# Tile order, small copies and the decays' chain in the start of a DeltaNet/MoBA block kernel

## The chip, the cores and the metric

The kernel runs on one core of one Trainium2 chip. The metric is the device time of a whole execution in microseconds (us), the median of several runs. The profile is of one execution of the same program.

## What is computed

One decoder block over 256 tokens of 1024 channels, all in float32. `x` is RMS-normalised to `h`, and one projection of `h` gives everything else:

```python
h = rms_norm(x, norm_pre_w)
proj = jnp.einsum('bsd,df->bsf', h, w_in)
qkv_a, z_a, beta_a, dec_a, qkv_b, z_b, gate_logits = ...
qkv_a = jax.nn.silu(causal_depthwise_conv(qkv_a, conv_w))        # 4 taps, per channel
beta = jax.nn.sigmoid(beta_a)
g = -jnp.exp(dn_a_log) * jax.nn.softplus(dec_a + dn_dt_bias)      # the decays
oa = gated_delta_rule(qa, ka, va, g, beta)                        # 8 heads of 128, chunks
ya = rms_norm(oa, dn_onorm_w) * silu(z_a)
ob = moba_attention(qb, kb, vb, rel_bias)                         # 256 tokens: one causal block
yb = ob * silu(z_b)
merged = sigmoid(gates_a) * (ya @ w_branch[0]) + sigmoid(gates_b) * (yb @ w_branch[1])
out = x + rms_norm(merged @ w_out, norm_post_w)
```

## The kernel before

Every large product is made in three parts. Weights and activations are split into a high part, rounded to the fp32r type, and the remainder: `w_hi`, `w_lo`, `h_hi`, `h_lo`. A product is `h_hi w_hi + h_lo w_hi + h_hi w_lo`, three passes over the same bank of PSUM. Weights come in tiles of 128 x 1024 (512 KB), one DMA each on SyncE's queue, into four slots (`raw`). ScalarE makes the high part (`split_hi`), VectorE the remainder (`split_lo`), TensorE does the three passes. A tile is loaded once the remainder of the tile four before it has left its slot.

The whole program is written out by hand, engine by engine, over one counter `S`: `n = S // 3` is the tile, `part = S % 3` the pass. In each step `S` every engine does first `gates(S)` (the small work for beta and decays), then the work on key tiles (`key_front`), and more, and ScalarE ends `part == 1` with the cast of tile `n + 2`, VectorE ends `part == 2` with its remainder. Each engine takes its instructions strictly in that order, and semaphores tie the engines together.

The first sixteen tiles are named by a string. K is a tile of the key projection of one DeltaNet head (8 blocks of 128 rows x 128 columns of `w_in`, out 128 channels x 256 tokens), V one of the attention's value projection (two blocks of 128 rows x 512 columns, for two of the eight parts of `h`; four V tiles make one group of 512 columns, in banks `bE` and `bF`).

```python
FIRST = "KVKKVKKVKKVKVVVV"
```

A K tile with index `j` among the K tiles goes to bank `j % 2` (`third`), and `bank_free` makes TensorE wait until the taps of key tile `j - 2` have read that bank: `pe.wait_ge(s_tap, 3 * (j - 1))`. For a key tile, ScalarE copies the bank times the fourth tap to `acc`, VectorE adds three shifted taps (`conv`, line 974): two in the step in which the tile is done, the third in the next. ScalarE's tanh and a last step on VectorE (line 987) give `kT_all`, which TensorE later transposes (`key_tokens`, the table `TOKENS` says at which `S`).

The start: `x` is normalised, 16 transposes (line 1266) turn it to channels x tokens in PSUM (`x_T`, `h` in eight parts), ScalarE rounds each part to `h_hi` (line 652), VectorE makes `h_lo` (line 926). `first_tile` (line 1332) is tile 0, here a K tile: 24 matmuls of 256 columns in an order that follows those parts, with the last four transposes among them. Its cast is done by VectorE (`first_hi`), its remainder by GpSimd. Tile 1's cast follows on ScalarE behind all eight roundings, then the cast of the small weights `wbd` (16 columns for beta and decays); VectorE has the first half of tile 1's remainder, then the remainder of `wbd`, then the other half.

Beta and decays: TensorE's `gates` at `S == 4` (16 matmuls, line 1291), a copy on ScalarE to `bd_T` (line 662), two transposes at `S == 6`. At `S == 7` VectorE has `bd_lo`, `bd`, `gt[:, 1]` and the copy `brow` (lines 943 to 951), ScalarE tanh, absolute value, two exponentials and a logarithm, which needs another table (lines 665 to 673), and GpSimd the chain between them (lines 525 to 541). VectorE sums at `S == 8` (line 960), and TensorE makes the cumulative sums at `S == 11` (lines 1307 to 1309).

## Time and profile before

| | |
|---|---|
| median of 3 runs | 354.02 us (353.72 to 354.14) |
| the profiled execution | 354.62 us |
| its span in the profile | 352.8 us |
| TensorE matmul busy | 345.2 us, 98% |
| VectorE | 269.7 us, 76% |
| ScalarE | 220.5 us, 62% |
| GpSimd | 61.0 us, 17% |
| HBM read | 60.41 MB, 176 GB/s over the span with what is written |

The span runs from the first to the last instruction of the program; the execution's time holds 1.8 us more around it. In the rows, PE is TensorE's matmuls, PEld its weight loads, DVE VectorE, ACT ScalarE, POOL GpSimd. Busy time of matmuls is modelled at their ends, and neighbours overlap in the records; where one matmul follows the other, the chain of waits shows what each group really adds.

### The profile page before, as it was taken

What the parts mean: (1) busy time and instruction counts of PE and PEld (TensorE: products, weight loads), DVE (VectorE), ACT (ScalarE), POOL (GpSimd) and SP (SyncE); (2) the same over time, 40 slices, a digit from 0 to 9 for tenths busy, and PEclk for the clock granted to TensorE, in tenths of its full rate; (3) what the DMA queues carried; (4) which work ended last, traced back from release to release, by engine and by line L of the source; (5) the groups of instructions that cost most, each with busy time, mean ns of one, the idle gap of its engine ahead of it and who ended that gap; (6) DMA issues with size and microseconds to landing.
All of it is one profiled execution on the core that took longest, in us unless ns stands there. A gap on an engine that the chain in (4) does not pass through costs nothing.

```text
span 352.8 us, 7457 instructions
## 1 busy us (share of the span) xinstructions
PE 345.2 (98%) x2753; PEld 332.2 (94%) x2753; DVE 269.7 (76%) x565; ACT 220.5 (62%) x499; POOL 61.0 (17%) x112
## 2 busy tenths in 40 slices
PE   8999999999999999999999999999999999999993
PEld 6889998999999999999999999999999999999882
DVE  4869897499986868978789797887967557588644
ACT  4778895455466667686866867677667655444421
POOL 2535535500033000300203011030200201000011
PEclk9999999999999999999999999999999999999999
DMA  7958948996799564655555565655555556775703
GB/s 233 274 140 225 304 125 201 236 289 171 209 248 218 134 180 126 163 133 153 146 150 149 131 170 129 171 132 146 143 159 143 171 158 181 208 240 186 260 32 119
DMA packets 100321, 62.48 MB, mean 177 GB/s; under 512 B 4692, under 2 KB 95230, under 8 KB 100286
## 3 DMA queue, kind: packets, MB, share of 16 engines
q1 hardware_dynamic: 98030, 58.59, 60.6%
q0 software_dynamic: 1072, 3.04, 3.0%
q10 hardware_dynamic: 1184, 0.39, 0.5%
q8 instruction: 22, 0.36, 0.4%
q14 instruction: 13, 0.11, 0.1%
HBM read 60.41 MB, written 1.59 MB: 176 GB/s over the span
## 4 chain that ended last, share of the span: by engine, by line
PE 97%; DVE 1%; issue 1%; POOL 0%; ACT 0%; DVEq 0%; POOLq 0%; ACTq 0%
PE banks L1347 67%; PE banks L1365 6%; PE banks L1560 6%; PE banks L1256 2%; PE banks L1445 1%; PE banks L1422 1%; PE banks L1462 1%; PE banks L1451 1%; PE banks L1332 1%; PE banks L1291 1%; PE banks L1507 1%; PE banks L1479 1%; PE banks L1483 1%; PE banks L1512 1%; PE banks L1487 1%
## 5 line engine op out<-in xcount | busy, mean ns | idle before, releaser
L890 DVE TENSOR_TENSOR w_lo<-raw,w_hi 128x1024 fp32r<-128x1024 f32 x102 | 124.1, 1218 | 44.4 <-ACT w_hi L637 43.9
L637 ACT CAST w_hi<-raw 128x1024 fp32r<-128x1024 f32 x103 | 107.5, 1047 | 10.0 <-PE banks L1560 5.5
L1347 PE MATMUL banks<-h_hi,w_hi 128*128 128x256 f32 x568 | 81.4, 286 | 0.0
L1347 PE MATMUL banks<-h_hi,w_lo 128*128 128x256 f32 x568 | 76.6, 278 | 0.0
L1347 PE MATMUL banks<-h_lo,w_hi 128*128 128x256 f32 x568 | 76.6, 278 | 0.0
L1347 PEld LDWEIGHTS banks<-h_hi,w_hi 128*128 128x128 f32 x568 | 71.0, 189 | 0.3
L1347 PEld LDWEIGHTS banks<-h_hi,w_lo 128*128 128x128 f32 x568 | 69.9, 188 | 0.0
L1347 PEld LDWEIGHTS banks<-h_lo,w_hi 128*128 128x128 f32 x568 | 69.9, 188 | 0.0
L974 DVE SCALAR_TENSOR_TENSOR acc<-banks,vec,acc 128x255 f32<-128x255 f32 (+2 forms) x72 | 34.5, 479 | 4.0 <-ACT acc L761 2.1
L587 POOL TENSOR_TENSOR so<-so,rnq 128x2 f32<-128x2 f32 x8 | 2.6, 328 | 162.8 <-ACT junk L828 162.8
L761 ACT ACTIVATE acc<-banks,vec 128x256 f32<-128x256 f32 x16 | 7.6, 474 | 18.7 <-PE banks L1347 18.7
L1347 PE MATMUL banks<-y_hi,w_hi 128*128 128x256 f32 x128 | 17.7, 281 | 0.0
L1347 PE MATMUL banks<-y_hi,w_lo 128*128 128x256 f32 x128 | 17.2, 277 | 0.0
L1347 PE MATMUL banks<-y_lo,w_hi 128*128 128x256 f32 x128 | 17.2, 277 | 0.0
L1347 PEld LDWEIGHTS banks<-y_hi,w_hi 128*128 128x128 f32 x128 | 15.8, 188 | 0.0
L1347 PEld LDWEIGHTS banks<-y_hi,w_lo 128*128 128x128 f32 x128 | 15.8, 188 | 0.0
L1347 PEld LDWEIGHTS banks<-y_lo,w_hi 128*128 128x128 f32 x128 | 15.8, 188 | 0.0
L1560 PE MATMUL banks<-w_hi,h_lo 128*128 128x512 f32 x32 | 12.6, 395 | 0.0
L1560 PE MATMUL banks<-w_lo,h_hi 128*128 128x512 f32 x32 | 12.5, 392 | 0.0
L1560 PE MATMUL banks<-w_hi,h_hi 128*128 128x512 f32 x32 | 12.4, 389 | 0.0
L765 ACT COPY bT<-banks 128x256 f32<-128x256 f32 x16 | 5.9, 371 | 9.3 <-PE banks L1347 9.2
L744 ACT CAST h_hi<-th_E 128x256 fp32r<-128x256 f32 x8 | 3.2, 406 | 12.1 <-DVE th_E L1190 12.1
(243 smaller groups left out, 548.3 us busy)
## 6 DMA issues: line engine op xcount, KB each, us to landing
raw<-in_w_in_dram SPq DMA_DIRECT2D x79, 512.0 KB, 4.0
raw<-in_w_branch_dram SPq DMA_DIRECT2D x16, 512.0 KB, 3.7
raw<-in_w_out_dram SPq DMA_DIRECT2D x8, 512.0 KB, 3.3
xin<-in_x_dram SPq DMA_DIRECT2D x2, 512.0 KB, 3.9
th_E<-g_rows POOLq DMA_DIRECT2D x2, 512.0 KB, 6.6
bias<-bias_rows POOLq DMA_DIRECT2D x1, 1024.0 KB, 8.2
raw<-in_x_dram SPq DMA_DIRECT2D x2, 512.0 KB, 4.4
out_dram<-xin SPq DMA_DIRECT2D x4, 256.0 KB, 2.0
```

Of the source, the lines that this page charges most:

```text
L637: nc.scalar.copy(w_hi[:, t % SLOTS, :], raw[:, t % SLOTS, :]).then_inc(s_hi, 1)
L761: ac(acc[:, t, :], ps, ACT.Copy, scale=tap(CONV - 1, 2 * t, h)).then_inc(s_tap0, 1)
L765: nc.scalar.copy(bT[:, t - 2, :], ps).then_inc(s_bT, 1)
L890: v.tensor_tensor(w_lo[:, t % SLOTS, cols], raw[:, t % SLOTS, cols], w_hi[:, t % SLOTS, cols].bitcast(F32), ALU.subtract).then_inc(s_lo, 1)
L974: v.scalar_tensor_tensor(out=acc[:, a, i:], in0=ps[:, 0:SEQ - i], scalar=tap(CONV - 1 - i, w, h), in1=acc[:, a, i:], op0=ALU.mult, op1=ALU ...
L1256: mm(bank[6][:, 0:SEQ], acc[:, 0, 0:P], acc[:, 0, :], start=True, stop=True)
L1291: last = mm(bA[0:4 * HEADS, 0:SEQ], wbd2[:, k, :], h_part[:, k, :], start=k == 0 and h_part is h_hi, stop=k == KT - 1 and h_part is h_lo)
L1332: last = mm(ps, (w_lo if which[1] == "l" else w_hi)[:, 0, P * k:P * k + P], (h_lo if which[0] == "l" else h_hi)[:, k, :], start=i == 0, st ...
L1347: last = mm(ps, w, r, start=part == 0 and k == 0, stop=part == 2 and k == KT - 1)
L1365: last = mm(((bE, bF), (bB, bE))[group][c], left, right, start=q == 0 and kk == 0 and part == 0, stop=q == 3 and kk == 1 and part == 2)
L1422: last = mm((bA, bC)[j % 2][:, P * c:P * c + P], k, k, start=True, stop=True)
L1560: last = mm(bank[2 + 2 * c + e], m[:, k, P * c:P * c + P], w[:, (OUT0 + k) % SLOTS, 512 * e:512 * e + 512], start=k == 0 and m is m_hi and ...
```

## The change

Tiles 0 and 1 change places: tile 0 is now a V tile, tile 1 the first K tile. `first_tile` makes the V tile's twelve matmuls of 512 columns, which need two of the eight parts of `h`, with the last six transposes among them; ten stand ahead. The eight parts in PSUM lie in other banks. The cast of tile 1 stands on ScalarE between the sixth and the seventh rounding, and VectorE's remainder of `wbd` ahead of tile 1's remainder. The constants `ones` and `tri` are loaded behind the fourth tile of weights and not ahead of the third. Key tile 0's work begins at `S == 6` and not at `S == 3`, its transposes move from `S == 10` to 12. The copy to `bd_T` is written at `S == 4` ("the projection's copy"), ahead of the cast of tile 3, together with the exponential of `alog`. GpSimd's chain of nine instructions on the decays is now VectorE's, in `gates` at `S == 7`. The diff, with one line around each piece:

```diff
@@ -51,7 +51,7 @@
-FIRST = "KVKKVKKVKKVKVVVV"
+FIRST = "VKKKVKKVKKVKVVVV"
 K_TILES = [n for n, kind in enumerate(FIRST) if kind == "K"]
@@ -69,7 +69,7 @@
-TOKENS = {10: 0, 16: 1, 19: 2, 24: 3, 27: 4, 32: 5, 35: 6, 41: 7}
+TOKENS = {12: 0, 16: 1, 19: 2, 24: 3, 27: 4, 32: 5, 35: 6, 41: 7}
 SIM = {28: 0, 29: 1, 30: 2, 31: 3, 36: 4, 37: 5, 42: 6, 43: 7}
@@ -216,7 +216,7 @@
-        x_T = [bank[(1, 2, 3, 5, 6, 7)[k % 6]][:, SEQ * (k // 6):SEQ * (k // 6) + SEQ] for k in range(KT)]
+        x_T = [bank[(1, 2, 3, 5, 0)[k % 5]][:, SEQ * (k // 5):SEQ * (k // 5) + SEQ] for k in range(KT)]
@@ -410,16 +410,16 @@
             for half in range(2):
-                part = slice(KT // 2 * half, KT // 2 * half + KT // 2)
-                sp.dma_start(raw[:, 0, :].rearrange("p (k n) -> p k n", k=KT)[:, part], w_tile(COL_K)[:, part]
+                sp.dma_start(raw[:, 0, 512 * half:512 * half + 512], w_in[P * half:P * half + P, COL_VB:COL_VB + 512]
                              ).then_inc((s_w0_in, s_raw[0])[half], 16)
             first_load(1)
-            sp.dma_start(cst[:, P:], consts[:, P:]).then_inc(s_cst, 16)
             sp.dma_start(wbd[:], w_in[:, COL_BD:COL_B].rearrange("(k p) n -> p k n", p=P)).then_inc(s_bd_w, 16)
                 first_load(n)
+                if n == 3:
+                    sp.dma_start(cst[:, P:], consts[:, P:]).then_inc(s_cst, 16)
             for g in range(EARLY):
@@ -518,28 +518,9 @@
-            pool.wait_ge(s_ga, 1)
+            pool.wait_ge(s_ga, 2)
             pool.tensor_scalar(gt[:, 11], gt[:, 0], -0.125, -0.125, ALU.mult, ALU.add).then_inc(s_beta, 1)
             pool.wait_ge(s_beta, 1)
-            pool.wait_ge(s_ga, 3)
-            pool.tensor_scalar(gt[:, 4], gt[:, 3], 1.0, 1.0, ALU.mult, ALU.add).then_inc(s_gs, 1)
-            pool.wait_ge(s_gs, 1)
-            pool.tensor_scalar(gt[:, 6], gt[:, 4], 1.0, -1.0, ALU.mult, ALU.add).then_inc(s_gs, 1)
-            pool.wait_ge(s_gs, 2)
-            pool.tensor_tensor(gt[:, 7], gt[:, 3], gt[:, 6], ALU.subtract).then_inc(s_gs, 1)
-            pool.wait_ge(s_gs, 3)
-            pool.tensor_tensor(gt[:, 8], gt[:, 1], gt[:, 2], ALU.add).then_inc(s_gs, 1)
-            pool.wait_ge(s_gs, 4)
-            pool.tensor_scalar(gt[:, 10], gt[:, 8], 0.5, 0.0, ALU.mult, ALU.add).then_inc(s_gs, 1)
-            pool.wait_ge(s_gs, 5)
-            pool.tensor_tensor(gt[:, 10], gt[:, 10], gt[:, 7], ALU.add).then_inc(s_gs, 1)
-            pool.wait_ge(s_gs, 6)
-            pool.wait_ge(s_ga, 4)
-            pool.tensor_scalar(tiny[:, 24:32], tiny[:, 16:24], -1.0, 0.0, ALU.mult, ALU.add).then_inc(s_gs, 1)
-            pool.wait_ge(s_gs, 7)
-            for c in range(NC):
-                pool.tensor_tensor(gt[:, 7, c], gt[:, 10, c], tiny[:, 24:32], ALU.mult).then_inc(s_gs, 1)
-                pool.wait_ge(s_gs, 8 + c)
             pool.wait_ge(s_brow, 1)
@@ -650,26 +631,27 @@
                 ac(h_hi[:, k, :], x_T[k], ACT.Copy, scale=vec[:, R_PRE + k:R_PRE + k + 1]).then_inc(s_h_hi, 1)
-            sa.wait_ge(s_hi, 1)
-            split_hi(1, 1, 1)
+                if k == 5:
+                    sa.wait_ge(s_hi, 1)
+                    split_hi(1, 1, 1)
             sa.wait_ge(s_bd_w, 16)
-                if S == 5:
+                if S == 4:
                     sa.wait_ge(s_bd_m, 1)
                     nc.scalar.copy(bd_T, bA[0:4 * HEADS, 0:SEQ]).then_inc(s_bd_t, 1)
+                    sa.wait_ge(s_small, 32)
+                    ac(tiny[:, 16:24], alog[:], ACT.Exp).then_inc(s_ga, 1)
                 elif S == 7:
                     ac(gt[:, 2], gt[:, 1], ACT.Abs).then_inc(s_ga, 1)
-                    sa.wait_ge(s_ga, 2)
+                    sa.wait_ge(s_ga, 3)
                     ac(gt[:, 3], gt[:, 2], ACT.Exp, scale=-1.0).then_inc(s_ga, 1)
-                    sa.wait_ge(s_small, 32)
-                    ac(tiny[:, 16:24], alog[:], ACT.Exp).then_inc(s_ga, 1)
-                    sa.wait_ge(s_gs, 1)
+                    sa.wait_ge(s_gs, 4)
                     ac(gt[:, 5], gt[:, 4], ACT.Ln).then_inc(s_ga, 1)
@@ -927,11 +909,11 @@
                     first_hi(1)
-            ve.wait_ge(s_lo, 2)
-            first_lo(1, 0, s_lo)
             ve.wait_ge(s_bd_hi, 1)
                             ALU.subtract).then_inc(s_bd_s, 1)
+            ve.wait_ge(s_lo, 2)
+            first_lo(1, 0, s_lo)
             first_lo(1, 1, s_lo)
@@ -949,10 +931,26 @@
                     v.tensor_copy(brow, bC[0:HEADS, 0:BIAS_W]).then_inc(s_brow, 1)
+                    ve.wait_ge(s_ga, 1)
+                    v.tensor_scalar(tiny[:, 24:32], tiny[:, 16:24], -1.0, None, ALU.mult).then_inc(s_gs, 1)
+                    ve.wait_ge(s_ga, 3)
+                    v.tensor_tensor(gt[:, 8], gt[:, 1], gt[:, 2], ALU.add).then_inc(s_gs, 1)
+                    ve.wait_ge(s_gs, 2)
+                    v.tensor_scalar(gt[:, 10], gt[:, 8], 0.5, None, ALU.mult).then_inc(s_gs, 1)
+                    ve.wait_ge(s_ga, 4)
+                    v.tensor_scalar(gt[:, 4], gt[:, 3], 1.0, None, ALU.add).then_inc(s_gs, 1)
+                    ve.wait_ge(s_gs, 4)
+                    v.tensor_scalar(gt[:, 6], gt[:, 4], -1.0, None, ALU.add).then_inc(s_gs, 1)
+                    ve.wait_ge(s_gs, 5)
+                    v.tensor_tensor(gt[:, 7], gt[:, 3], gt[:, 6], ALU.subtract).then_inc(s_gs, 1)
+                    ve.wait_ge(s_gs, 6)
+                    v.tensor_tensor(gt[:, 10], gt[:, 10], gt[:, 7], ALU.add).then_inc(s_gs, 1)
+                    ve.wait_ge(s_gs, 7)
+                    for c in range(NC):
+                        v.tensor_tensor(gt[:, 7, c], gt[:, 10, c], tiny[:, 24:32], ALU.mult).then_inc(s_gs, 1)
                 elif S == 8:
                     ve.wait_ge(s_ga, 5)
-                    ve.wait_ge(s_gs, 7)
                     for c in range(NC):
@@ -1271,15 +1269,12 @@
             pe.wait_ge(s_pre_xb[0], 1)
-            pe.wait_ge(s_vec, 1)
-            for k in range(4, 6):
-                turn(0, k)
+            turn(0, 4)
             pe.wait_ge(s_pre_x[1], 1)
             pe.wait_ge(s_pre_xb[1], 1)
-            for k in range(4, 6):
-                turn(1, k)
+            turn(1, 4)
@@ -1310,27 +1305,35 @@
-
-                ps = bank[0][:, 0:SEQ]
-                order = ("hh0 hh1 lh0 hh2 lh1 hh3 lh2 hl0 hh4 lh3 hl1 hh5 lh4 hl2 hh6 lh5 hl3 hh7 lh6 hl4 "
-                         "hl5 hl6 hl7 lh7").split()
+                def first_turn(k):
+
+                    pe.wait_ge(s_h_lo, k - 4)
+                    for c in range(NC):
+                        turn(c, k)
+
+                def first_products(kk, left, right):
+
+                    for c in range(NC):
+                        mm((bE, bF)[c], left[:, kk, P * c:P * c + P], right[:, 0, 512 * kk:512 * kk + 512],
+                           start=kk == 0 and left is h_hi and right is w_hi, stop=False)
+
+                pe.wait_ge(s_vec, 1)
                 pe.wait_ge(s_w0_hi, 1)
-                for i, which in enumerate(order):
-                    k = int(which[2])
-                    if which == "hh4":
-                        pe.wait_ge(s_hi, 1)
-                    if which in ("lh0", "lh1"):
-                        pe.wait_ge(s_h_lo, k + 1)
-                        for c in range(NC):
-                            turn(c, 6 + k)
-                    if which[0] == "l":
-                        pe.wait_ge(s_h_lo, k + 1)
-                    else:
-                        pe.wait_ge(s_h_hi, k + 1)
-                    if which[1] == "l":
-                        pe.wait_ge(s_lo, 1 + k // 4)
-                    last = mm(ps, (w_lo if which[1] == "l" else w_hi)[:, 0, P * k:P * k + P],
-                              (h_lo if which[0] == "l" else h_hi)[:, k, :], start=i == 0, stop=i == 23)
+                pe.wait_ge(s_h_hi, 1)
+                first_products(0, h_hi, w_hi)
+                first_turn(5)
+                first_products(0, h_lo, w_hi)
+                pe.wait_ge(s_hi, 1)
+                pe.wait_ge(s_h_hi, 2)
+                first_products(1, h_hi, w_hi)
+                first_turn(6)
+                first_products(1, h_lo, w_hi)
+                first_turn(7)
+                pe.wait_ge(s_lo, 1)
+                first_products(0, h_hi, w_lo)
+                pe.wait_ge(s_lo, 2)
+                for c in range(NC):
+                    last = mm((bE, bF)[c], h_hi[:, 1, P * c:P * c + P], w_lo[:, 0, 512:], start=False, stop=False)
                 last.then_inc(s_tile, 1)
@@ -1342,6 +1345,8 @@
                 for k in range(KT):
+                    if n == 1 and part < 2:
+                        pe.wait_ge((s_h_hi, s_h_lo)[part], k + 1)
                     w = (w_lo if part == 2 else w_hi)[:, slot, P * k:P * k + P]
@@ -1373,6 +1378,8 @@
                     j = K_TILES.index(n)
+                    if j == 0:
+                        pe.wait_ge(s_h_lo, 5)
                     if j >= 2:
                 elif n < HEAD0:
```

VectorE around loop step 7, before (`acc<-banks` are the taps of key tile 0, of 255, 254 and 253 columns; `w_lo` the remainders of tiles 2, 3 and 4):

```order
L890 TENSOR_TENSOR w_lo<-raw,w_hi 128x1024
L974 SCALAR_TENSOR_TENSOR acc<-banks,vec,acc 128x255
L974 SCALAR_TENSOR_TENSOR acc<-banks,vec,acc 128x254
L974 SCALAR_TENSOR_TENSOR acc<-banks,vec,acc 128x253
L890 TENSOR_TENSOR w_lo<-raw,w_hi 128x1024
L987 SCALAR_TENSOR_TENSOR kT_all<-tacc,acc 128x256
L943 COPY bd_lo<-banks 128x32
L945 TENSOR_TENSOR bd<-banks,bd_lo 128x32
L949 TENSOR_TENSOR gt<-bd,dtb 128x8 x2
L951 COPY pt<-banks 8x384
L957 TENSOR_TENSOR gt<-gt,tiny 128x8 x2
L960 TENSOR_TENSOR tab<-gt 128x16
```

And now, from the copy `brow` (`pt<-banks`) on; the second tap of key tile 0 and the steps `bd_lo`, `bd` and `gt[:, 1]` stand right ahead of it:

```order
L933 COPY pt<-banks 8x384
L935 TENSOR_SCALAR tiny<-tiny 128x8
L937 TENSOR_TENSOR gt<-gt 128x16
L939 TENSOR_SCALAR gt<-gt 128x16
L941 TENSOR_SCALAR gt<-gt 128x16
L943 TENSOR_SCALAR gt<-gt 128x16
L945 TENSOR_TENSOR gt<-gt 128x16
L947 TENSOR_TENSOR gt<-gt 128x16
L950 TENSOR_TENSOR gt<-gt,tiny 128x8 x2
L972 SCALAR_TENSOR_TENSOR acc<-banks,vec,acc 128x253
L955 TENSOR_TENSOR gt<-gt,tiny 128x8 x2
L958 TENSOR_TENSOR tab<-gt 128x16
```

Between the second tap of key tile 0 and the third (253 columns) there now stand the old steps of loop step 7 and the nine instructions that were GpSimd's (lines 935 to 950); tile 3's remainder has moved ahead of the taps and `kT_all` of key tile 0 behind tile 4's.

TensorE from tile 3 on, before, with what each row waits for (`h,w` are passes of the tile, `kT_all` the transposes of key tile 0, `cst,tab` and `tab,cst` the cumulative sums):

```order
L1347 MATMUL banks<-h_hi,w_hi 128x256 [waits s_hi,s_tap]
L1347 MATMUL banks<-h_hi,w_hi 128x256 x7
L1411 MATMUL banks<-cst,kT_all 128x128 [waits s_h_lo,s_kact]
L1411 MATMUL banks<-cst,kT_all 128x128
L1347 MATMUL banks<-h_lo,w_hi 128x256 x8
L1307 MATMUL banks<-cst,tab 8x128 [waits s_cst,s_brow,s_g]
```

And now:

```order
L1352 MATMUL banks<-h_hi,w_hi 128x256 [waits s_hi,s_tap]
L1352 MATMUL banks<-h_hi,w_hi 128x256 x7
L1352 MATMUL banks<-h_lo,w_hi 128x256 x8
L1302 MATMUL banks<-cst,tab 8x128 [waits s_cst,s_brow,s_g]
L1302 MATMUL banks<-cst,tab 8x128
L1303 MATMUL banks<-tab,cst 128x16
L1304 MATMUL banks<-tab,cst 128x16
L1352 MATMUL banks<-h_hi,w_lo 128x256 [waits s_lo]
L1352 MATMUL banks<-h_hi,w_lo 128x256 x7
L1418 MATMUL banks<-cst,kT_all 128x128 [waits s_h_lo,s_kact]
```

Tile 3's wait on `s_tap` is the same in both, for the third tap of key tile 0. The transposes of that key tile have moved from the middle of tile 3 to its end, behind the cumulative sums.

## Rows read from the trace of the kernel before

**Rows 1.** The page: busy time by engine, clock in 40 slices, the chain's shares.

```profile
PE 345.2 (98%) x2753; PEld 332.2 (94%) x2753; DVE 269.7 (76%) x565; ACT 220.5 (62%) x499; POOL 61.0 (17%) x112
...
PEclk9999999999999999999999999999999999999999
...
PE 97%; DVE 1%; issue 1%; POOL 0%; ACT 0%; DVEq 0%; POOLq 0%; ACTq 0%
```

**Rows 2.** Timeline of PE: start, duration in us, count, [idle before <-releaser].

```profile
7.52 1.53 PE L1266 MATMUL banks<-cst,xin 128*128 128x128 f32 x12
...
21.07 1.11 PE L1347 MATMUL banks<-h_hi,w_hi 128*128 128x256 f32 x8
...
23.80 0.60 PE L1307 MATMUL banks<-cst,tab 128*8 128x128 f32 x4 [0.46 <-DVE tab L960]
```

**Rows 3.** Chain of waits, 14 to 29 us: start, us, what (by the ends).

```profile
14.31 1.83 PE banks L1291 x16
16.14 1.83 PE banks L1365 x8
...
24.95 1.04 PE banks L1347 x8
25.99 2.77 PE banks L1365 x12
29.70 0.22 PE banks L1411 x2
```

**Rows 4.** Timeline of ACT, 8 to 22.5 us.

```profile
8.61 3.02 ACT L652 ACTIVATE h_hi<-banks,vec 128x256 fp32r<-128x256 f32 x8 [0.56 <-PE banks L1266]
...
14.48 1.05 ACT L637 CAST w_hi<-raw 128x1024 fp32r<-128x1024 f32 x1 [1.71 <-DMA raw<-in_w_in_dram]
...
16.24 1.05 ACT L637 CAST w_hi<-raw 128x1024 fp32r<-128x1024 f32 x1 [0.34 <-DMA raw<-in_w_in_dram]
17.20 0.36 ACT L662 COPY y<-banks 32x256 f32<-32x256 f32 x1
...
20.69 0.19 ACT L671 ACTIVATE tiny<-alog 128x8 f32<-128x8 f32 x1
20.90 1.28 ACT L673 ACT_TABLE_LOAD   x1
```

**Rows 5.** Timeline of DVE, 9 to 27 us.

```profile
9.21 0.48 DVE L926 SCALAR_TENSOR_TENSOR h_lo<-banks,vec,h_hi 128x256 fp32r<-128x256 f32 x1 [0.85 <-ACT h_hi L652]
...
16.71 1.51 DVE L974 SCALAR_TENSOR_TENSOR acc<-banks,vec,acc 128x255 f32<-128x255 f32 x3
18.13 1.22 DVE L890 TENSOR_TENSOR w_lo<-raw,w_hi 128x1024 fp32r<-128x1024 f32 x1
...
19.60 0.19 DVE L943 COPY bd_lo<-banks 128x32 f32<-128x32 f32 x1
...
20.21 0.54 DVE L951 COPY pt<-banks 8x384 f32<-8x384 f32 x1
23.02 0.28 DVE L957 TENSOR_TENSOR gt<-gt,tiny 128x8 f32<-128x8 f32 x2 [2.27 <-POOL tiny L538]
...
26.58 0.15 DVE L964 COPY tab<-banks 128x16 f32<-128x16 f32 x1
26.77 0.17 DVE L966 TENSOR_TENSOR gt<-banks,tab 128x8 f32<-128x8 f32 x1
26.85 0.17 DVE L967 TENSOR_SCALAR ng<-tab 128x16 f32<-128x16 f32 x1
```

**Rows 6.** Timeline of POOL: the last links of its chain.

```profile
22.71 0.20 POOL L538 TENSOR_SCALAR tiny<-tiny 128x8 f32<-128x8 f32 x1
23.00 0.48 POOL L541 TENSOR_TENSOR gt<-gt,tiny 128x8 f32<-128x8 f32 x2
```

**Rows 7.** Stretches at the end: busy PE, PEld, DVE, ACT, POOL, PEclk, DMA, GB/s.

```profile
347.00:348.00 1.00, 0.09 (x1) 0.00 (x0) 0.09 (x1) 0.69 (x2) 0.00 (x0) 1.00 0.00 0
...
350.50:351.00 0.50, 0.00 (x0) 0.00 (x0) 0.00 (x0) 0.00 (x0) 0.00 (x0) 1.00 0.93 348
```

## The prediction

> **What bounds the kernel now.** I read the page first: TensorE is busy for 98% of the span and the chain of waits is 97% TensorE [rows 1], so only places where TensorE pauses, or where its work grows, can change the time. Both places are early. Until the end of the first tile it runs on what the other engines have just made of `h` (first part rounded at 8.61, first remainder at 9.21 [rows 4, 5]), and at 23.80 us it stood for 0.46 us before the cumulative sums, released by VectorE's sum of the decays [rows 2]. From 24.95 us on the chain of waits is one matmul group behind another [rows 3]: no gap is left there to gain. So I walk both orders up to the cumulative sums of the decays and compare where TensorE stands behind them; what it is late or early there, the end is late or early.
>
> Prices of TensorE's work come from the chain: eight 512-column matmuls 1.83 (so a pass of four, or of eight with 256 columns, 0.91 to 0.95), a whole tile 2.77, the sixteen for beta and decay 1.83, two transposes 0.22, the cumulative sums 1.15 (23.80 to 24.95) [rows 3].
>
> **The change, part by part. Total work.** The first tile is now 12 matmuls of 512 columns and the second 24 of 256, before it was the other way round; 16 transposes stay 16. Nothing is added to TensorE, nothing removed.
>
> *Start.* Five transposes instead of six stand ahead of the first of the second half. Twelve took 1.53 [rows 2], so 0.13 each: ScalarE's first rounding moves from 8.61 [rows 4] to 8.49. TensorE then starts its products at 9.1, and since the value tile needs only the first two of `h`'s eight parts it runs through them: six groups of two 512-column matmuls (0.46 each) and three pairs of transposes (0.22). VectorE's first remainder (9.69 before, by the 9.21 and 0.48 of its row, so 9.57 now) holds the first pair to 9.62 [rows 5]. 9.62 + 3 x 0.22 + 5 x 0.46 gives 12.6. The projection's tile 1 can start there if its cast is done: it now stands on ScalarE behind the sixth rounding. Eight roundings in 3.02 [rows 4] are 0.36 apart, so it runs from 10.7 to 11.8. The two roundings behind it end at 12.5, the cast of the small weights at 12.7, VectorE's last remainder at 13.1, the small weights' remainder (which now goes ahead of tile 1's) at 13.3. TensorE does the first pass of tile 1 to 13.5 and waits for none of them; sixteen small matmuls to 15.4, and the two other passes to 17.2. Before, the chain had the same work done at 17.97 (16.14 and 1.83) [rows 3]. **This part gains 0.8 us for TensorE.**
>
> *Constants behind the fourth weights.* Their load is 128 KB of the 512 KB tiles' stream. ScalarE waited 1.71 us for tile 2's weights and 0.34 for tile 3's, which landed at 14.48 and 16.24 [rows 4], 1.76 apart; a quarter of that is 0.4, so both land 0.4 earlier. The constants themselves are wanted at 23.80 first and land near 17: no cost. Tile 3's cast can use only part of it: ScalarE's copy of the small result and the exponential of `alog` now stand ahead of it, and the copy waits for the sixteen matmuls (15.4 + 0.1). With 0.36 and 0.19 for the two (the next overlapping a little) [rows 4] the cast starts at 16.0 instead of 16.24 and ends at 17.05.
>
> *The chain on VectorE.* This decides. Tile 3's remainder runs from 17.05 and lets the next start at 18.2 (1.22, the next overlapping by some 0.07) [rows 5]. Key tile 0 now comes from tile 1, done at 17.2, its copy on ScalarE at 17.75, so its first two taps start at 18.2, and 18.7 (three taps 1.51) [rows 5]. Then, **ahead of the third tap**, stand the gates' steps of loop step 7: `bd_lo` at 19.1 (the third tap stood near 17.73, the remainder after it at 18.13: 0.40), `brow` 0.61 later at 19.7 (19.60 to 20.21), whose row of 0.54 holds the engine to 20.2 [rows 5]. Behind it are the nine moved ones. The trace has them on GpSimd only, where two take 0.48 and one 0.20, so 0.28 apart [rows 6]. On VectorE 16-column instructions that wait for the one before stand 0.19 apart (26.58 to 26.77), others 0.08 (26.77 to 26.85) [rows 5]. Five of the steps wait for VectorE itself (0.2 each), the others don't (four, 0.1 each with the tap): 1.4 in all. Bounds are 9 x 0.08 = 0.7 and 9 x 0.28 = 2.5; I take 1.4, by the rows of VectorE itself. So the third tap starts at 21.6 and ends at 22.05. ScalarE's table load hides: tanh, absolute value and exponential run from 19.5 to 20.2, the load takes 1.28 [rows 4] and the logarithm ends by 21.8; the decays are summed by 22.5, against 23.8 before [rows 2]. **The chain itself is 1.3 us earlier.**
>
> *The new wait.* Tile 3 is the third of the projection, writes the same bank as the first and so waits for all three taps of key tile 0. Before, these were over at 18.22 (16.71 and 1.51) [rows 5], and TensorE came to tile 3 at 21.07 [rows 2]. Now TensorE comes to it at 17.2 + 0.24 + 2.74 = 20.15 and finds the third tap behind the whole chain: it stands until 22.1, **1.95 us**. Queued behind that wait are two passes of tile 3 (1.9, to 24.0) and the cumulative sums (the decays have been ready since 22.5; 1.15, to 25.15). The two transposes of key tile 0 that stood ahead of the sums are moved behind, so 0.22 is still owed: 25.37 against 24.95, **0.4 us late**.
>
> *Afterwards.* ScalarE's second table load now precedes tile 5's cast, which ends at 25.7, wanted at 28.8. VectorE has tile 4's remainder from 22.7, key tile 0 at 24.4, the taps of key tile 1 at 24.85, tile 5's remainder at 26.95; before, that remainder followed 26.85 [rows 5]. So VectorE and ScalarE are where they were, and TensorE, 0.4 behind, waits for neither. The nine steps fall into what was a 2.27 us pause of VectorE [rows 5].
>
> *A rule on the clock.* The granted clock shows nine tenths or more in all 40 slices [rows 1], and in the tail, where the last matmul ends at 347.1, it is still 1.00 (2.4 GHz) past 350.5 [rows 7]; so a pause of 1.95 costs its own length, no more. The Trainium skill, "TensorE: Matmul & The Clock Gate", section "HAM oscillation — how this bites in real kernels", says that TensorE's pauses between bursts of matmuls can drop the clock, so that the next burst starts slow. By that the sum would be larger (rivals).
>
> **Sum.** +0.4 on the profiled execution's 354.62 is 355.0. That execution stands 0.60 over the median of the three runs, 354.02, so the forecast for the median is **354.4 us**. A measurement of this kernel can tell about 0.2%, 0.71 us, from no change: the forecast is inside it.
>
> **Rivals.**
> *1, slower: the third tap comes later still.* Everything on VectorE up to it passes straight to TensorE. If tile 3 lands no earlier than 16.24, its cast starts 0.24 later, and if the five waiting steps cost GpSimd's 0.28 and a little more, 0.45 later: 354.4 + 0.7 = 355.1. It decides for slower by over 0.2% once the tap starts after 21.9. For it: the chain has a dozen links, each able to slip. Against: rows of VectorE show 0.19 to 0.23. 28%.
> *2, slower: the clock falls in the pause.* Then each microsecond of matmuls at 1.2 GHz costs one more; a single value tile (2.77 in the chain [rows 3]) would make it 354.4 + 2.8 = 357.2. Against it stand over 3 us of pause at full clock in the tail [rows 7]. 3%. This is the page's rule of above.
> *3, faster: the tap is not what holds tile 3.* If the steps pass in 0.7, the tap ends 0.7 sooner: 353.7, still within 0.2%. For more, the tap would have to be done by the time TensorE comes, 20.15: then tile 3's passes end at 22.05, the sums start at the decays' 22.5 and end at 23.65, with the owed 0.22 at 23.87, 1.1 us early: 352.9. The order of the instructions speaks against it. 7%.
> *4, the change does nothing.* If the load and the order of the first tile win no time, TensorE's early 0.8 is lost, which the pause of 1.95 covers; but `bd` and with it the taps are then late and it ends as rival 1. It is counted there.
>
> **Numbers.** Forecast 62%, within 0.2%; rivals 1 and 2 31%, slower; rival 3 7%, counted faster. The range takes in the fast bound of the steps with some reserve (353.6) and rival 1 with 0.2 more (355.3); left out are the clock and the whole of rival 3.
>
> **What would show it.** In the profile of the changed kernel: TensorE idle for about 1.9 us before the first pass of tile 3 at 22.1, released by VectorE's 253-column tap; that tap at 21.6, nine small steps before it in 1.4; tile 1 finished near 17.2; the sum of the decays at 22.4; cumulative sums without a wait; granted clock 1.00. If the pause is under 1 us, or is not released by that tap, the walk is wrong; if pauses stand behind 25 us, the part on afterwards is.

## The result: slower by 2.9 us, and the profile after

| | before | changed |
|---|---|---|
| median of the comparison (12 executions each) | 354.08 us | 356.97 us |
| lowest to highest | 353.72 to 354.59 | 355.38 to 360.14 |
| profiled execution (its span) | 354.62 (352.8) | 355.38 (353.6) |

The ratio is 1.0080 (95% interval 1.0065 to 1.0094): slower by 0.8%, 2.9 us, where 0.4 was forecast. The spread matters as much as the median. Five of the twelve executions of the changed kernel have a mean granted clock of 0.998 and took 355.38 to 355.98; the other seven have 0.986 to 0.995 and took 356.96 to 360.14. (The clock also falls behind the last matmul of every profiled execution, so that a mean of 0.995 alone does not tell the two groups apart; the time does.) The profiled one is the fastest of the twelve. So there are two questions: why is an execution at full clock 1.6 us slower than before, and what happens in the others.

The page, against [rows 1]. At full clock the profile shows only that TensorE is no longer the whole chain:

```profile
PE 343.4 (97%) x2753; PEld 330.9 (94%) x2753; DVE 270.5 (76%) x574; ACT 220.8 (62%) x499; POOL 58.9 (17%) x103
...
PEclk9999999999999999999999999999999999999999
...
PE 92%; SPq 2%; DMA 2%; DVE 2%; ACT 0%; issue 0%; POOL 0%; DVEq 0%; POOLq 0%; ACTq 0%
```

TensorE's timeline, against [rows 2, 3] (start, us, count, [idle before <-releaser]):

```profile
12.62 1.10 PE L1352 MATMUL banks<-h_hi,w_hi 128*128 128x256 f32 x8
...
16.27 1.07 PE L1352 MATMUL banks<-h_hi,w_lo 128*128 128x256 f32 x8
...
22.56 1.21 PE L1352 MATMUL banks<-h_hi,w_hi 128*128 128x256 f32 x8 [1.97 <-DVE acc L972]
...
24.64 0.60 PE L1302 MATMUL banks<-cst,tab 128*8 128x128 f32 x4
...
26.78 1.18 PE L1370 MATMUL banks<-w_hi,h_hi 128*128 128x512 f32 x4
```

The steps of the walk are all there: tile 1 begins at 12.62 and its last pass at 16.27 (over near 17.2), then TensorE stands 1.97 us ahead of tile 3, released by VectorE's tap, and the cumulative sums (24.64) wait for nothing. The pause is as long as forecast (1.95) by luck: both of its ends are late. TensorE is through with tile 2 at 20.59 and not at 20.15. (A key tile takes longer than the 2.74 of the walk: tile 2 began at 18.14 and tile 3 at 21.07 before, 2.93 us.) And tile 3 starts at 22.56 and not at 22.1. Only the second of these moves what follows. VectorE's timeline, against [rows 5], shows what the tap stood behind:

```profile
18.71 0.99 DVE L972 SCALAR_TENSOR_TENSOR acc<-banks,vec,acc 128x255 f32<-128x255 f32 x2
19.62 0.18 DVE L925 COPY bd_lo<-banks 128x32 f32<-128x32 f32 x1
...
20.23 0.54 DVE L933 COPY pt<-banks 8x384 f32<-8x384 f32 x1
20.70 0.15 DVE L935 TENSOR_SCALAR tiny<-tiny 128x8 f32<-128x8 f32 x1
...
21.87 0.24 DVE L950 TENSOR_TENSOR gt<-gt,tiny 128x8 f32<-128x8 f32 x2
22.03 0.47 DVE L972 SCALAR_TENSOR_TENSOR acc<-banks,vec,acc 128x253 f32<-128x253 f32 x1
```

The nine moved steps take 1.33 us (20.70 to 22.03; 1.4 was forecast). The whole stretch stands 0.4 to 0.5 later than in the walk. ScalarE's timeline, against [rows 4], has the reason, and SyncE's issues have the reason behind that:

```profile
14.72 1.05 ACT L618 CAST w_hi<-raw 128x1024 fp32r<-128x1024 f32 x1 [2.01 <-DMA raw<-in_w_in_dram]
...
16.49 1.05 ACT L618 CAST w_hi<-raw 128x1024 fp32r<-128x1024 f32 x1 [0.34 <-DMA raw<-in_w_in_dram]
```

```profile
6.39 2.51 SPq L417 DMA_DIRECT2D alog<-in_dn_a_log_dram  x1
8.95 0.43 SPq L418 DMA_DIRECT2D dtb<-in_dn_dt_bias_dram  x1
9.42 1.06 SPq L397 DMA_DIRECT2D raw<-in_w_in_dram  x2
10.52 2.40 SPq L422 DMA_DIRECT2D cst<-in_consts_dram  x1
```

Tiles 2 and 3 landed at 14.72 and 16.49, 0.25 later than before, not 0.4 earlier. In the profile of before SyncE's issues read:

```profile
6.93 0.77 SPq L419 DMA_DIRECT2D alog<-in_dn_a_log_dram  x1
7.74 0.43 SPq L420 DMA_DIRECT2D dtb<-in_dn_dt_bias_dram  x1
8.22 2.48 SPq L397 DMA_DIRECT2D raw<-in_w_in_dram  x2
```

Both kernels have, among these loads, an issue that holds SyncE for about 2 us or more. Before, it fell on the second of tiles 2 and 3 (the other issues here take 0.43 to 0.8, the two together 2.48), when tile 2 was already on its way from 8.22. Now it falls on the 4 KB of `alog`, ahead of both tiles, which are issued from 9.42 on.

### The profile page after: what moved, and what is told of

It reads as the page before. It is cut to its first block, busy times and chain, and to the rows that moved or that the text cites. A ratio compares the mean times of both kernels' runs of the same rounds, so it can differ in the third digit from the quotient of the medians.

```text
span 353.6 us, 7446 instructions
## 1 busy us (share of the span) xinstructions
PE 343.4 (97%) x2753; PEld 330.9 (94%) x2753; DVE 270.5 (76%) x574; ACT 220.8 (62%) x499; POOL 58.9 (17%) x103
## 4 chain that ended last, share of the span: by engine, by line
PE 92%; SPq 2%; DMA 2%; DVE 2%; ACT 0%; issue 0%; POOL 0%; DVEq 0%; POOLq 0%; ACTq 0%
PE banks L1352 67%; PE banks L1567 6%; PE banks L1370 5%; DMA raw<-in_w_in_dram 2%; PE banks L1452 1%; PE banks L1429 1%; PE banks L1469 1%; PE banks L1458 1%; SPq L417 1%; PE banks L1514 1%; PE banks L1519 1%; PE banks L1490 1%; PE banks L1494 1%; PE banks L1486 1%; PE banks L1507 1%; PE banks L1526 1%
## 5 line engine op out<-in xcount | busy, mean ns | idle before, releaser
L1352 PE MATMUL banks<-h_hi,w_hi 128*128 128x256 f32 x576 | 82.4, 286 | 2.0 <-DVE acc L972 2.0
L1352 PE MATMUL banks<-h_hi,w_lo 128*128 128x256 f32 x576 | 77.5, 277 | 0.0
L1352 PE MATMUL banks<-h_lo,w_hi 128*128 128x256 f32 x576 | 77.5, 277 | 0.0
L1352 PEld LDWEIGHTS banks<-h_hi,w_hi 128*128 128x128 f32 x576 | 72.0, 189 | 2.6 <-DVE acc L972 2.2
L1352 PEld LDWEIGHTS banks<-h_lo,w_hi 128*128 128x128 f32 x576 | 70.8, 188 | 0.0
L1352 PEld LDWEIGHTS banks<-h_hi,w_lo 128*128 128x128 f32 x576 | 70.8, 188 | 0.0
L1352 PE MATMUL banks<-y_hi,w_lo 128*128 128x256 f32 x128 | 17.2, 277 | 0.0
L1352 PE MATMUL banks<-y_lo,w_hi 128*128 128x256 f32 x128 | 17.2, 277 | 0.0
```

The source lines that it names most:

```text
L1352: last = mm(ps, w, r, start=part == 0 and k == 0, stop=part == 2 and k == KT - 1)
```

## Experiments

The profile pointed at the pause ahead of tile 3. **Theory A**: the pause is the cause of both parts, by its length and because the clock falls behind it in more than half of the executions. **Theory B**: the spread has nothing to do with the pause. Each run's median and its ratio to the kernel before (with the 95% interval) come from executions of both on the same chip. Pauses and starts are read from one profiled execution of each run.

**1. The pause filled.** Sixteen idle products ahead of the wait, into a bank that nobody reads then:

```diff
+ if j == 2:
+     for i in range(16):
+         mm(bD[:, 0:SEQ], h_hi[:, 0, 0:P], h_hi[:, 0, :], start=True, stop=True)
  pe.wait_ge(s_tap, 3 * (j - 1))
```

> The changed kernel with 16 matmuls of 256 columns into an unused bank right ahead of tile 3's wait for the third tap; their result is not used. Theory A (TensorE's pause of 1.97 us lets the clock fall in most executions, and that is what the median of 356.97 holds over the profiled 355.38): the pause shrinks to some 0.2 us, the end of the wait stays where it was, every execution is at 355.4 within 0.5 us and the mean clock is 0.998 in all. Theory B (the spread comes from the start: the order of loads and when they land): nothing changes, 355.4 to 360 and clocks down to 0.986.

355.63 us (355.31 to 356.03, 12 executions), 1.0040 [1.0027, 1.0054]; every mean clock 0.995 or more, as in the kernel before. Tile 3 starts where it did:

```profile
22.53 1.19 PE L1352 MATMUL banks<-h_hi,w_hi 128*128 128x256 f32 x8
```

The work added takes the spread away and 1.3 us off the median: more work, less time. The times are as theory A expected; B would have kept the spread.

**2. The third tap ahead of the chain** (all three taps of key 0 in one step):

```diff
- conv(bank[a], a, 1, j, 3 * j, (1, 2))
+ conv(bank[a], a, 1, j, 3 * j, (1, 2) if j else (1, 2, 3))
```

> The changed kernel with the third tap of key tile 0 right behind the first two, ahead of the gates' steps. Walk: the taps end at 20.1, TensorE comes to tile 3 at 20.4 and does not wait; the sum of the decays stays at 22.8 to 23.0, so TensorE waits some 0.6 us ahead of the cumulative sums, as before the change, and stands behind them 1.6 us earlier than in the changed kernel. Theory A: 353.8 us, narrow, clock 0.998. Theory B: 355.3 median, still spread by some us.

355.49 (355.31 to 355.94), 1.0040 [1.0026, 1.0053], clocks 0.995 or more. The spread is gone, the 353.8 did not come. TensorE goes straight into tile 3 at 20.23 and then waits, as its timeline shows:

```profile
23.44 0.60 PE L1302 MATMUL banks<-cst,tab 128*8 128x128 f32 x4 [1.12 <-DVE tab L958]
...
25.98 0.44 PE L1418 MATMUL banks<-cst,kT_all 128*128 128x128 f32 x2 [0.35 <-DVE kT_all L985]
...
33.30 0.41 PE L1418 MATMUL banks<-cst,kT_all 128*128 128x128 f32 x2
```

The next value tile starts at 26.17, 0.35 later than in the profile of before (25.82). More is lost at the transposes at 33.30, where the distance to before grows to 0.75 (the matmuls behind them start at 33.47, before at 32.72). In run 7 the profile names a wait of 0.24 us for ScalarE's copies `k_all` at this place. The span ends 0.8 later. ScalarE's timeline of run 2 shows what stands behind the wait at 25.98: the second table load, which the key's tanh needs, now follows the logarithm, because key tile 0 comes one tile later.

```profile
21.29 1.28 ACT L655 ACT_TABLE_LOAD   x1
...
23.75 1.28 ACT L677 ACT_TABLE_LOAD   x1
25.05 0.42 ACT L677 ACTIVATE tacc<-acc 128x256 f32<-128x256 f32 x1
```

**3. A pause put into the kernel before** (`pe.wait_ge(s_gs, 8)` ahead of tile 3, an event of GpSimd's chain).

> The kernel before, with one more wait of TensorE ahead of tile 3: for the eighth step of GpSimd's chain on the decays. Nothing else of the change. TensorE stands there from 21.1 to 23.3, 2.2 us, and the wait ahead of the cumulative sums goes; without the clock that is +1.6: 355.7. Theory A: the clock falls in many executions, the median is 356.5 or more and spread over some us, with clocks under 0.998. Theory B: 355.7 within 0.5, clock 0.998 in all.

355.64 (355.08 to 357.49), 1.0049 [1.0030, 1.0067]. The pause came out at 1.19 us. Ten executions stand at 355.1 to 356.0; two at 357.49, with clocks of 0.993 and 0.995. Theory A's median of 356.5 or more did not come; the pause was only half of the 2.2 us expected. The two executions jump as the changed kernel's do, in a kernel that has nothing else of the change. But 2 of the 115 executions of the kernel before that were measured beside all these runs stand apart with a lower clock as well (355.64 and 356.81, clocks 0.991 and 0.987). So two of twelve point to theory A and do not show it; what shows it are runs 1, 5 and 11.

**4. As 2, with tile 2 issued ahead of the small loads** (`first_load(2)` moved before `wbd`).

> The third tap ahead as in the run before, and the loads of the small weights and of the two small vectors behind tile 2's on SyncE's queue. In the changed kernel SyncE's issue of the vector alog took 2.51 us and tile 2 was issued at 9.42 instead of 8.22. If small rows behind a key tile fill the queue and hold the issue, tile 2 lands some 2 us earlier than 14.72 and tile 3 at 15.5 or sooner instead of 16.49; the small weights may land later than 12.4. The taps then start 0.3 earlier and the time is 353.4. If the small weights are late, the sixteen small matmuls wait and it is 353.8 or more. Theory B would have the spread shrink here and not in the run before.

355.69 (355.27 to 356.32), 1.0043 [1.0026, 1.0059]. Tile 2 was there by 13.36 without a wait, but SyncE's hold moved to `wbd` (6.41, 2.98 us) and tile 3 landed at 16.86, later than in the change. Neither of the times expected (353.4, 353.8) came: the waits ahead of the sums and of the first transposes are 1.10 and 0.34, as in run 2. With the value tile first the hold stays at 6.4 us, whichever load stands there.

**5. A longer pause**: tile 3 waits for tile 4's remainder too (`pe.wait_ge(s_lo, lo_done(4))`).

> The changed kernel with tile 3 waiting in addition for the remainder of tile 4, which is over near 24.5 us, so that TensorE pauses about 4.0 us (20.6 to 24.5) in place of 1.97. As a delay alone this is 2.0 us: 357.4 to 357.7 in every execution. Theory A (the pause itself lets the granted clock fall, more surely the longer it is): most or all executions show a mean clock under 0.995 and stand 1 to 5 us above 357.5; median 358.5 to 362; if the profiled one is among them, a stretch soon after the pause is granted 0.5 and its matmuls take twice as long. Theory B (the clock has nothing to do with the pause): 357.5 with a clock of 0.995 or more in nearly all.

359.52 (359.03 to 359.77, 4 executions), 1.0144 [1.0129, 1.0159]; all four clocks 0.989 to 0.993. The profiled execution, clock in stretches (the columns as in [rows 7]) and TensorE's timeline:

```profile
24.00:25.00 1.00, 0.01 (x1) 0.02 (x1) 0.93 (x1) 0.99 (x2) 0.00 (x0) 1.00 0.04 16
25.00:26.00 1.00, 1.00 (x5) 1.00 (x6) 0.56 (x2) 1.00 (x3) 0.00 (x0) 0.56 0.00 1
26.00:27.00 1.00, 1.00 (x7) 1.00 (x7) 0.93 (x3) 0.70 (x1) 0.00 (x0) 0.50 0.77 135
27.00:28.00 1.00, 1.00 (x6) 1.00 (x6) 0.32 (x1) 0.42 (x1) 0.00 (x0) 0.50 1.12 338
28.00:29.00 1.00, 1.00 (x8) 0.66 (x6) 0.00 (x0) 0.00 (x0) 0.00 (x0) 0.73 0.18 51
```

```profile
24.99 1.98 PE L1352 MATMUL banks<-h_hi,w_hi 128*128 128x256 f32 x8 [4.38 <-DVE w_lo L872]
```

The pause is 4.38 us. The clock is at 1.00 through it and falls to 0.50 (1.2 GHz) once TensorE is at work again; eight matmuls take 1.98 us instead of 1.21.

**6. Half of the filler** (eight products).

> The changed kernel with eight filler matmuls of 256 columns (0.13 each, 1.04 us) ahead of tile 3's wait: the pause is about 0.9 us, and tile 3 starts where it did. Theory A (the clock falls by the length of the pause): hardly any execution under 0.995, median 355.5 to 355.8. If any pause will do: several of twelve under 0.995 and a median above 356.

355.82 (355.58 to 356.25, 5 executions), 1.0042 [1.0029, 1.0056], clocks 0.995 or more. The trace gives a pause of 1.41 us, not 0.9, since tile 3 landed late in it (17.14).

**7. The change with the chain back on GpSimd** (the nine steps in the change's order, only their move to VectorE undone).

> The changed kernel with the nine steps of the decays' chain back on GpSimd, in the order the change has them. The third tap comes behind brow, over by 21.3: TensorE pauses 0.5 to 0.9 us at tile 3 instead of 1.97. The nine steps cost 0.28 each there, so that the sum of the decays is ready at 23.5 to 23.9, when tile 3 is through. If moving the chain to VectorE is what costs (pause and clock): 355.3 to 355.7 without a clock under 0.995, median 1.3 us less than the changed kernel's. If the chain on VectorE gains more than it costs: 356.5 or more.

355.04 (354.85 to 355.39, 12 executions), 1.0022 [1.0014, 1.0031], clocks 0.995 or more. TensorE's and VectorE's timelines:

```profile
21.68 1.19 PE L1353 MATMUL banks<-h_hi,w_hi 128*128 128x256 f32 x8 [1.11 <-DVE acc L973]
```

```profile
23.50 0.17 DVE L959 TENSOR_TENSOR tab<-gt 128x16 f32<-128x16 f32 x1 [0.41 <-POOL gt L540]
```

The pause is 1.11 us and the sum of the decays is ready at 23.7, just as tile 3's second pass ends. So within the new tile order the move of the chain to VectorE costs 2.0 us of the 2.9 (0.0058 of the ratio; the falls of the clock are in it), and on GpSimd it would have hidden.

**8 to 11. The changed kernel again**, one profiled execution each, to see a fall of the clock in a profile.

> The changed kernel once more, one look: 7 of its 12 executions had a mean clock of 0.995 or less, so with about even chance this one shows where the clock falls. Theory A: a stretch granted about 0.5 that begins within 10 us behind the pause at 20.6 to 22.6, and the rest at 1.00. If the fall lies elsewhere, theory A is wrong.

> The changed kernel once more, one look, to find an execution in which the clock falls (7 of 12 had a lower mean clock, the two profiled so far had not). Theory: in such a one the granted clock reads 0.5 for some 3 us from just behind the pause ahead of tile 3, its matmuls take nearly twice as long, and the end is 1.3 us or more later; everywhere else it is 1.00.

> As the look before: the changed kernel, to find an execution in which the clock falls, with the same expectation.

> As the two looks before: the changed kernel, to find an execution in which the clock falls, with the same expectation.

355.77, 355.72, 355.55 (clocks 0.998 to 0.999) and 357.53 (0.994). The fourth has it, as the stretches and TensorE's timeline show:

```profile
22.00:23.00 1.00, 0.00 (x0) 0.00 (x0) 0.90 (x6) 0.99 (x3) 0.77 (x1) 1.00 1.01 358
23.00:24.00 1.00, 0.78 (x4) 0.78 (x5) 0.52 (x5) 0.98 (x3) 0.00 (x0) 0.77 0.19 55
24.00:25.00 1.00, 1.00 (x6) 1.00 (x6) 1.00 (x1) 1.00 (x1) 0.00 (x0) 0.50 0.06 25
25.00:26.00 1.00, 1.00 (x7) 1.00 (x6) 0.50 (x2) 0.99 (x4) 0.00 (x0) 0.50 0.00 0
26.00:27.00 1.00, 1.00 (x6) 0.70 (x6) 0.96 (x3) 0.97 (x2) 0.00 (x0) 0.53 0.58 95
27.00:28.00 1.00, 1.00 (x9) 0.76 (x8) 0.56 (x3) 0.38 (x1) 0.00 (x0) 1.00 1.06 306
```

```profile
23.23 1.84 PE L1352 MATMUL banks<-h_hi,w_hi 128*128 128x256 f32 x8 [2.31 <-DVE acc L972]
24.86 1.91 PE L1352 MATMUL banks<-h_lo,w_hi 128*128 128x256 f32 x8
...
28.95 1.18 PE L1370 MATMUL banks<-w_hi,h_hi 128*128 128x512 f32 x4
```

From the start of tile 3 to the next value tile it takes 5.72 us (23.23 to 28.95), at full clock 4.22 (22.56 to 26.78): the fall costs 1.5 us. The stretches on both sides of it are at 1.00, so this is the place and the price. The pauses of the four are 2.22, 1.83, 2.04 and 2.31 us. The clock fell behind the longest, but one of 2.22 kept it: within this range the length alone hardly decides.

**12. The chain alone**: the kernel before with its nine steps on VectorE behind `brow`.

> The kernel before with the nine steps of the chain moved to VectorE behind brow, and nothing else. There the taps of key tile 0 are already over when the chain comes, so it holds up nothing that TensorE waits for; the decays are summed by 22.8 and the wait of 0.46 ahead of the cumulative sums is gone. Theory: 0.46 less than before, 353.6, clock 0.995 or more. Rival (as in the second experiment another bound stands behind, such as ScalarE's second table load ahead of the first key's transposes): within 0.2 of before, with a wait of 0.3 or more behind the sums.

354.01 against 354.02, 0.9998 [0.9989, 1.0007]. It does what was said on VectorE: the decays' sum is at 22.44 here,

```profile
22.44 0.17 DVE L959 TENSOR_TENSOR tab<-gt 128x16 f32<-128x16 f32 x1
```

and it brings nothing, where 353.6 was expected. No wait of TensorE is left in its profile behind 10 us, so the rival's new wait is not there either. Run 14 says why.

**13. The chain, the constants behind the fourth weights and the early exponential**, all of the change but the new tile order and what belongs to it.

> As the kernel with the chain alone moved, and in addition the constants loaded behind the fourth weights and the exponential of alog done ahead of the tanh, as the change has them: all of the change but the value tile first. Before waits at tiles 2 and 3 for nothing, so an earlier or a later landing by some 0.4 costs or gains nothing: equal to the chain alone, 353.6, within 0.3. If the load order matters by itself: more than 0.4 apart from it.

353.91, 0.9996 [0.9988, 1.0005]: equal to run 12, as expected. Here tiles 2 and 3 do land earlier (casts at 13.57 and 15.23; in run 12 at 14.09 and 15.83), and it is worth nothing, since TensorE waits for neither.

**14. The kernel before again**, one profiled execution.

> The kernel before once more, one look: its profiled execution stood 0.60 above the median of the three runs. If that is the landing of tiles 2 and 3 behind SyncE's issues, this one shows them landing at another time and TensorE's first passes of those tiles moved with them; if it lies elsewhere (the end, or the issue of the last stores), the early part is the same to 0.1.

354.32. TensorE's timeline, against the wait of 0.46 in [rows 2]:

```profile
21.25 1.11 PE L1347 MATMUL banks<-h_hi,w_hi 128*128 128x256 f32 x8
...
23.50 0.60 PE L1307 MATMUL banks<-cst,tab 128*8 128x128 f32 x4
```

There is no wait at all ahead of the sums. Tile 3 landed at 15.93 instead of 16.24, and with it the copy behind its cast, the whole chain of the decays and its sum (23.27) are 0.3 earlier. The execution that the prediction was worked out from had a wait that this one does not have, and ended 0.3 us later.

**15. A value tile in third place.** If TensorE's lead from the first tile is real, it must be kept from standing in a wait. Order VKKVKKVKKVKKVVVV, taps as in 2, and the logarithm, the decays' sum and the cumulative sums two steps later. The edit in short, without the steps of VectorE and ScalarE that move along:

```diff
- FIRST = "VKKKVKKVKKVKVVVV"
+ FIRST = "VKKVKKVKKVKKVVVV"
- TOKENS = {12: 0, 16: 1, 19: 2, 24: 3, 27: 4, 32: 5, 35: 6, 41: 7}
+ TOKENS = {12: 0, 16: 1, 22: 2, 24: 3, 30: 4, 32: 5, 38: 6, 41: 7}
  (ScalarE)  S == 7: tanh, abs, exp
+ (ScalarE)  S == 9: the logarithm
- (PE)       S == 11: the cumulative sums
+ (PE)       S == 13: the cumulative sums
```

> The changed kernel with a value tile in third place (order VKKVKKVKKVKKVVVV), so that TensorE has 2.8 us of work that waits for no tap; with all three taps of key 0 together; with the logarithm two loop steps later, behind key 0's tanh and the cast of tile 4, and the decays' sum, the cumulative sums and what follows them two steps later as well. Theory (the first tile's order does free 0.8 us of TensorE, and the change lost it again to its own waits): TensorE never waits behind 10 us, and the end is 0.7 to 0.8 earlier than before, 353.3, clock 0.995 or more. Rival (something else is late next, for example the casts of tiles 3 and 4 behind their late landing, or the fourth key tile behind its taps): one or two waits of 0.3 to 1 us between 15 and 45 us, 353.6 to 354.5.

354.62, 1.0014 [1.0005, 1.0023]: 0.1 above the rival's range (353.6 to 354.5), and with the rival's picture. TensorE's timeline has two waits, 0.79 us together, about the size of the lead. (Tile 2 starts 0.64 earlier than before in the profile of the result, 17.50 against 18.14, and 0.89 earlier in run 8 than in run 14.)

```profile
23.64 0.44 PE L1419 MATMUL banks<-cst,kT_all 128*128 128x128 f32 x2 [0.29 <-DVE kT_all L986]
...
25.50 0.60 PE L1303 MATMUL banks<-cst,tab 128*8 128x128 f32 x4 [0.50 <-DVE tab L959]
```

**16. These two places one step later** (`TOKENS` 13 for key 0, the sums at 14).

> The kernel with the value tile in third place, and two places moved one loop step (about 0.95 us of TensorE) later: the transposes of key 0, which waited 0.29 us for VectorE, and the cumulative sums with all that follows from them, which waited 0.50 us. Theory (these two waits are what kept the freed 0.8 us): TensorE waits for nothing between 10 and 45 us, and the end is 0.8 earlier than that kernel's, 353.8, that is 0.3 to 0.4 under before. Rival (ScalarE's and VectorE's later steps inherit the delay): new waits of 0.2 us or more behind 30 us, 354.2 to 354.8.

353.73 (353.43 to 354.10, 11 executions), 0.9986 [0.9977, 0.9995] against 354.10: the one version clearly below the kernel before, by 0.37 to 0.5 us (the difference of the medians, and the ratio). One wait of 0.16 is left.

```profile
25.93 0.60 PE L1303 MATMUL banks<-cst,tab 128*8 128x128 f32 x4 [0.16 <-DVE tab L959]
```

## Why the prediction was wrong

Right were the shape and most terms: the first tile's order (tile 1 done near 17.2), the nine steps (1.33 against 1.4), the wait that takes the others' place and its releaser, the sums without a wait, nothing waiting for tiles 4 and 5. Three steps failed.

1. **"So a pause of 1.95 costs its own length, no more."** This rested on one tail [rows 7] and gave rival 2 a chance of 3%. By their clocks and times 8 of 16 executions of the changed kernel had a fall; one of the eight is profiled. By length of the pause, as the profiled executions show it: 1.1 to 1.4 us (runs 2, 3, 4, 6, 7) 2 of 53, which the 2 of 115 of the kernel before do not clearly differ from; 1.8 to 2.3 (the changed kernel) 8 of 16; 4.4 (run 5) 4 of 4. One fall costs 1.5 us where it was seen in the changed kernel; the median stands 1.25 above the full-clock executions (356.97 and 355.72). The rule of the Trainium skill that was weighed there ("TensorE: Matmul & The Clock Gate", "HAM oscillation — how this bites in real kernels") is borne out: the burst behind the pause in run 11 is at 0.50 from 0.3 us after its start. Other tails would have warned. In run 6 the last matmul ends at 348.7 and the clock has fallen by 351; in run 8 (355.77 us) it ends at 348.3 and the clock falls past 353:

```profile
348.00:349.00 1.00, 0.74 (x4) 0.27 (x2) 0.00 (x0) 0.16 (x1) 0.00 (x0) 1.00 0.11 41
...
350.00:351.00 1.00, 0.00 (x0) 0.00 (x0) 0.67 (x2) 0.00 (x0) 0.49 (x1) 0.86 0.00 0
351.00:352.00 1.00, 0.00 (x0) 0.00 (x0) 1.00 (x2) 0.00 (x0) 0.00 (x0) 0.50 0.00 0
```

```profile
348.00:349.00 1.00, 0.27 (x2) 0.00 (x0) 0.00 (x0) 0.64 (x2) 0.00 (x0) 1.00 0.00 0
...
353.00:354.00 1.00, 0.00 (x0) 0.00 (x0) 0.00 (x0) 0.00 (x0) 0.00 (x0) 0.73 0.12 43
```

One pause in which the clock held says little about the next one of the same length. What decides between two executions of one program stays open.

2. **"Both land 0.4 earlier."** The bytes were counted, the issue was not. Tile 3's cast came at 16.49 instead of 16.0 (at 16.43 to 17.17 in runs 8 to 11), and everything down to the third tap with it: tile 3 started at 22.56 instead of 22.1. Size: 0.46. In the old order the term holds (run 13, 0.5 and 0.6 earlier than in run 12; the two profiles of the kernel before differ by 0.3 among themselves). Why SyncE's hold falls on `alog` with the value tile first, and on a weight tile otherwise, stays open.

3. **The credit of 0.46 for the wait ahead of the sums, carried to the median.** The sum was made against an execution 0.60 above the median and moved down by 0.60 whole, as if the offset lay elsewhere. Run 14 has no such wait and ends 0.3 earlier, so part of the offset is that wait. Run 12 removes the wait's cause and leaves the median where it was, so the median execution has none to give back. Between runs 14 and 8, both at full clock, the change is 1.48 at tile 3 (21.25 to 22.73) and 1.45 at the end (354.32 to 355.77). Size: 0.46.

From the forecast's 0.4: with 0.46 and 0.46 it is 1.3, against 1.64 between the median before and the full-clock executions (354.08 and 355.72); 0.3 is not accounted for step by step. Most of it may lie between the median execution of the kernel before and its profiled ones: run 14 too stands 0.24 above that median. With the clock's 1.25 it comes to 2.6 of the 2.9. Rival 1 had the right sign and place, but at most 0.7. "VectorE and ScalarE are where they were" held only because TensorE was late: run 2 shows the next bounds, 1.12, 0.35 and the one at 33.3 us, as soon as the tap is out of the way.

Not settled: why the same pause lets the clock fall in one execution and not in the next; the executions of 358.51 and 360.14 lose more than one fall of 1.5 us; and the two executions of the kernel before at 355.64 and 356.81 come from a program whose profiles have no long pause. None of these was caught in a profile.

## What to carry to other kernels

A pause of TensorE between two stretches of matmuls is not priced by its length alone: at about 2 us here it costs some 1.5 us more in half of the executions, and idle products that filled it took 1.3 us off the median. Before an idle gap is booked as a gain, look whether a second execution has it. When a chain of small steps is put on a faster engine, look first at what stands behind it in that engine's order: the same steps on GpSimd delayed nobody (run 7), and on VectorE in the old order neither (run 12).

## What had not been expected of the hardware

- The fall comes behind the pause, not in it: 1.00 to the end of 2.3 and 4.4 us of idle time, by the means of the stretches 0.50 from 0.3 and 0.1 us after TensorE resumed (23.23 and 24.99), and 1.00 again some 3 us later.
- Mostly at 0.50, eight matmuls of 256 columns took 1.84 to 1.98 us (1.07 to 1.21 at 1.00); a stretch of 4.22 us took 5.72 and, in run 5, 5.76 (24.99 to 30.75).
- SyncE's issue of a 4 KB load took 2.51 us (0.77 before) and of the 64 KB `wbd` 2.98 in run 4 (0.58 in the change), where a tile of 512 KB took 0.43 in run 4 (at 11.52): the size of a load does not set the time of its issue. What does is not shown.
